# Down projection of a two-layer decoder step: low parts of the weights on VectorE, sums read out one item earlier, additions spread over two products

## The reference

```
def ffn(x, norm_g, w_gu, w_down):
    h = rmsnorm(x, norm_g)
    g, u = jnp.split(h @ w_gu, 2, axis=-1)
    return x + (jax.nn.silu(g) * u) @ w_down
```

## Time and profile before

| | us |
|---|---|
| median of three runs (lowest, highest) | 2724.93 (2722.43, 2726.48) |
| profiled execution | 2711.63 |
| its span, first to last instruction | 2710.0 |
| TensorE matmul busy | 2627.9 (97%) |
| VectorE busy | 1598.3 (59%) |
| ScalarE busy | 1131.1 (42%) |
| GpSimd busy | 1248.2 (46%) |
| mean granted TensorE clock | 0.997 |

### The profile page before, as it was taken

The page is one execution under the profiler, slowest core; times in us unless marked ns, Lnnn a source line. Parts: engine busy times, 40 slices in busy tenths (PEclk is TensorE's granted clock), DMA queues, the critical chain, the costliest instruction groups (busy, mean ns, idle before and its releaser), DMA issues.

```text
span 2710.0 us, 51112 instructions
## 1 busy us (share of the span) xinstructions
PE 2627.9 (97%) x20404; PEld 2371.3 (88%) x20404; DVE 1598.3 (59%) x2435; ACT 1131.1 (42%) x2373; POOL 1248.2 (46%) x986
## 2 busy tenths in 40 slices
PE   8999999999999999999999999999999999999998
PEld 6866667666679899999999999978999999999998
DVE  3222257776563666766668861285376667666875
ACT  4022213666551644444433342175264444434335
POOL 2431000222232488778744651236257787775452
PEclk9999999999999999999999999999999999999999
DMA  7754310310433232322375331200322223228433
GB/s 231 207 166 154 92 32 12 105 33 2 137 110 138 69 101 84 113 93 93 101 261 182 85 90 41 54 2 17 105 68 98 97 85 117 93 95 309 134 83 104
DMA packets 256590, 283.78 MB, mean 105 GB/s; under 512 B 43098, under 2 KB 192655, under 8 KB 255506
## 3 DMA queue, kind: packets, MB, share of 16 engines
q1 hardware_dynamic: 245840, 247.84, 29.1%
q0 software_dynamic: 7616, 30.14, 3.6%
q10 hardware_dynamic: 2898, 2.54, 0.3%
HBM read 214.25 MB, written 71.32 MB: 105 GB/s over the span
## 4 chain that ended last, share of the span: by engine, by line
PE 63%; DVE 7%; issue 1%; ACT 1%; POOL 1%; DMA 1%; SPq 0%; DVEq 0%; ACTq 0%; POOLq 0%
PE ps L2541 32%; PE ps L3114 13%; PE ps L2342 8%; PE ps L2358 3%; DVE d_blo L3058 2%; DVE arena L3072 1%; PE ps L3438 1%; PE ps L3298 1%; PE ps L3419 1%; DVE part L2701 1%; PE ps L3402 1%; PE ps L2010 1%; PE ps L1998 1%; PE ps L2045 0%; DMA arena<-in_w_gate_up 0%
## 5 line engine op out<-in xcount | busy, mean ns | idle before, releaser
L2541 PE MATMUL ps<-part,block_hi 128*128 128x272 f32 x4768 | 793.6, 289 | 10.8 <-DVE spare_sb L2763 6.4
L2541 PEld LDWEIGHTS ps<-part,block_hi 128*128 128x128 f32 x4768 | 677.5, 189 | 11.6 <-DVE spare_sb L2763 6.8
L2541 PE MATMUL ps<-part,block_lo 128*128 128x272 f32 x2672 | 532.1, 290 | 0.0
L2829 POOL TENSOR_TENSOR block_lo<-arena,block_hi 128x512 fp32r<-128x512 f32 x296 | 443.7, 1529 | 53.4 <-ACT block_hi L2596 46.8
L2541 PEld LDWEIGHTS ps<-part,block_lo 128*128 128x128 f32 x2672 | 410.1, 190 | 1.0 <-issue 1.0
L3063 POOL TENSOR_TENSOR d_wlo<-arena,d_whi 128x512 fp32r<-128x512 f32 x154 | 248.0, 1630 | 249.5 <-ACT d_whi L3054 249.3
L3114 PE MATMUL ps<-d_bhi,d_whi 128*128 128x272 f32 x1232 | 258.3, 291 | 23.4 <-DVE arena L3201 12.8
L3114 PE MATMUL ps<-d_blo,d_whi 128*128 128x272 f32 x1232 | 256.5, 289 | 0.0
L3114 PE MATMUL ps<-d_bhi,d_wlo 128*128 128x272 f32 x1232 | 255.7, 289 | 0.0
L633 PE MATMUL ps<-arena 128*128 128x352 f32 (+1 forms) x768 | 240.8, 471 | 0.0
L2596 ACT CAST block_hi<-arena 128x512 fp32r<-128x512 f32 x296 | 167.1, 618 | 147.6 <-POOL arena L2844 86.1
(11 more groups left out here) (518 smaller groups left out, 4670.9 us busy)
## 6 DMA issues: line engine op xcount, KB each, us to landing
arena<-in_w_gate_up SPq DMA_DIRECT2D x176, 256.0 KB, 3.8
spare_sb<-a_keep SPq DMA_DIRECT2D x78, 272.0 KB, 2.8
arena<-a_keep SPq DMA_DIRECT2D x64, 272.0 KB
arena<-in_w_down SPq DMA_DIRECT2D x16, 1024.0 KB, 6.3
a_keep<-arena SPq DMA_DIRECT2D x58, 272.0 KB, 2.1
arena<-in_cache_nsa_slc_kv SPq DMA_DIRECT2D x112, 128.0 KB, 2.5
a_keep<-spare_sb SPq DMA_DIRECT2D x52, 272.0 KB, 2.0
arena<-in_cache_nsa_cmp_kv SPq DMA_DIRECT2D x109, 128.0 KB, 2.3
```

Source lines behind the costliest of these rows:

```text
L2541: mm = nc.tensor.matmul(ps[:, b + j, 0:QT], y, z[:, j * QT:(j + 1) * QT], start=first and m == 0, stop=last and m == 2)
L2829: p.tensor_tensor(block_of(q, "lo", a), block_f[q % 2]["lo", a], block_of(q, "hi", a).bitcast(F32), ALU.subtract).then_inc(sem("up_lo"), 1)
```

## The change

`low_w` takes the engine as an argument. GpSimd makes the low parts of the weights of items 0 to 5 alone; from item 6 on VectorE makes them, each right after the low part of the item's activations. VectorE evicts quads 0 and 1 after item j == 2 and quads 2 and 3 after item j == 3 of the next product; the weight sums of j = 1, 2, 3 are put off until these evictions are issued. ScalarE's copies of P1's banks move from j = 3, 4 to j = 2, 3. Two of the four `v_buf` pieces are now halves of `gate_even[0]`. Of the twelve `add_v`, four stay in P5 (j = 5 to 8, one each) and eight move to P3 (j = 5 to 8, two each). ScalarE's last four scalings and VectorE's four `low` move from between items 72 to 75 to behind the last item.

```
--- before.py
+++ after.py
@@ -2887,7 +2887,7 @@
         D_BANKS = (6, 0, 2, 4)
         D_SEGS, D_SEGS_LAST = ((0, 3), (3, 6), (6, 9), (9, PAIRS)), ((0, 3), (3, 6), (6, PAIRS))
         place = {"11": h0 + 12672, "21": h0 + 18304, "12": h0 + 23936}
-        v_buf = [rstd[:][:, 0:HT], rstd[:][:, HT:T], t2_buf, t3_buf]
+        v_buf = [rstd[:][:, 0:HT], rstd[:][:, HT:T], gate_even[0][:, 0:HT], gate_even[0][:, HT:]]
         stage_odd = [spare_sb[:, T:T + HT], spare_sb[:, T + HT:2 * T]]
 
         def stage(n):
@@ -3057,10 +3057,10 @@
             dve.wait_ge(*high_done("b", l, n))
             nc.vector.tensor_tensor(entry(n)[1], stage(n), entry(n)[0].bitcast(F32), ALU.subtract).then_inc(sem("d_blo"), 1)
 
-        def low_w(pool, l, n):
+        def low_w(e, engine, l, n):
             name, j = item(n)
-            pool.wait_ge(*high_done("w", l, n))
-            nc.gpsimd.tensor_tensor(entry(n)[3], stay(D_STAYS[name], j), entry(n)[2].bitcast(F32), ALU.subtract)\
+            e.wait_ge(*high_done("w", l, n))
+            engine.tensor_tensor(entry(n)[3], stay(D_STAYS[name], j), entry(n)[2].bitcast(F32), ALU.subtract)\
                 .then_inc(sem("d_wlo"), 1)
 
         def sum_w(e, engine, l, n):
@@ -3072,8 +3072,8 @@
             engine.tensor_tensor(stay(dst, j), stay(a, j), stay(b, j), op).then_inc(sem("d_sum"), 1)
 
         def down_pool(pool, l):
-            for n in range(ITEMS):
-                low_w(pool, l, n)
+            for n in range(RING):
+                low_w(pool, nc.gpsimd, l, n)
 
         SQUARES = [(u, 0) for u in range(QUADS)] + [(u, 1) for u in range(QUADS, KC)] + [(u, 1) for u in range(QUADS)] \
             + [(u, 0) for u in range(QUADS, KC)]
@@ -3145,11 +3145,11 @@
                 high_b(act, l, n)
                 high_w(act, l, n)
                 i, j = n // PAIRS, n % PAIRS
-                if i == 1 and j in (3, 4):
-                    if j == 3:
+                if i == 1 and j in (2, 3):
+                    if j == 2:
                         act.wait_ge(sem("up_a"), FC * (l + 1))
-                        act.wait_ge(*kept_z(l, PAIRS))
-                    for q in (range(QUADS - 1), (QUADS - 1,))[j - 3]:
+                        act.wait_ge(*kept_even(l, 0, EVENS[0]))
+                    for q in (2 * (j - 2), 2 * (j - 2) + 1):
                         act.wait_ge(*quad_done(l, 0, q))
                         nc.scalar.copy(two(v_buf[q]), product_banks(q)).then_inc(sem("d_copied"), 1)
                 if i in (2, 5) and 6 <= j < 10:
@@ -3160,8 +3160,8 @@
                     act.wait_ge(*item_used(l, LAST0 - 1))
                     for u in range(QUADS):
                         scaled(u, slice(0, T))
-                if n >= LAST0 + RING and n < LAST0 + RING + QUADS:
-                    scaled(QUADS + n - LAST0 - RING, slice(HT, T))
+            for u in range(QUADS, KC):
+                scaled(u, slice(HT, T))
 
             def finish(k):
                 act.wait_ge(*evicted(l, len(D_ORDER) - 1, k))
@@ -3189,6 +3189,8 @@
                     dve.wait_ge(*x_again(l, 0))
                 if name == "P7" and q == 0:
                     dve.wait_ge(*x_again(l, 1))
+                if name == "P5" and q == 0:
+                    dve.wait_ge(*x_again(l, 2))
                 if name == "P1":
                     dve.wait_ge(*copied(l, q))
                 if name == "P6":
@@ -3201,12 +3203,11 @@
                     ins = v.tensor_tensor(x, x, got, ALU.subtract if name == "P4" else ALU.add)
                 ins.then_inc(sem("d_evict"), 1)
 
-            def add_v(k):
-
-                q, (u, half) = k // 3, ((k // 3, 1), (QUADS + k // 3, 0), (QUADS + k // 3, 1))[k % 3]
-                if k == 0:
+            def add_v(q, u, half):
+
+                if u == 0:
                     dve.wait_ge(*x_again(l, 2))
-                dve.wait_ge(*evicted(l, 3, q))
+                dve.wait_ge(*evicted(l, 4 if u < QUADS else 3, q))
                 x = x_half(u, half)
                 v.tensor_tensor(x, x, v_buf[q], ALU.add).then_inc(sem("d_vadd"), 1)
 
@@ -3228,24 +3229,39 @@
                 v.scalar_tensor_tensor(out=h_lo[u], in0=xT[:, u], scalar=cols[:, g0 + u:g0 + u + 1],
                                        in1=h_hi[u].bitcast(F32), op0=ALU.mult, op1=ALU.subtract).then_inc(sem("h_lo"), 1)
 
-            for n in range(3, ITEMS):
-                low_b(dve, l, n)
+            def sums(n):
                 if 2 * PAIRS <= n + SUM_LEAD < LAST0:
                     dve.wait_ge(*low_done("w", l, n + SUM_LEAD - PAIRS))
                     sum_w(dve, v, l, n + SUM_LEAD)
+
+            for n in range(3, ITEMS):
+                low_b(dve, l, n)
+                if n == RING:
+                    dve.wait_ge(*low_done("w", l, RING - 1))
+                if n >= RING:
+                    low_w(dve, v, l, n)
                 i, j = n // PAIRS, n % PAIRS
+                if i == 0 or j not in (1, 2, 3):
+                    sums(n)
                 if i == 0 and 3 <= j < 7:
                     sum_pair(dve, l, PAIRS - 1, j - 3)
+                if i and j == 2:
+                    if i == 5:
+                        dve.wait_ge(*reached("d_vadd", 3 * QUADS * l + QUADS))
+                    if i == 6:
+                        dve.wait_ge(*reached("d_vadd", 3 * QUADS * (l + 1)))
+                    evict(i - 1, 0)
+                    evict(i - 1, 1)
                 if i and j == 3:
-                    if i == 5:
-                        dve.wait_ge(*reached("d_vadd", 3 * QUADS * (l + 1)))
-                    for q in range(QUADS - 1):
-                        evict(i - 1, q)
-                if i and j == 4:
-                    evict(i - 1, QUADS - 1)
-                if i == 4 and j >= 5:
-                    for k in range(2 * (j - 5), 2 * (j - 4)):
-                        add_v(k)
+                    evict(i - 1, 2)
+                    evict(i - 1, 3)
+                    for m in range(n - 2, n + 1):
+                        sums(m)
+                if i == 4 and 5 <= j < 5 + QUADS:
+                    add_v(j - 5, QUADS + j - 5, 1)
+                if i == 5 and 5 <= j < 5 + QUADS:
+                    add_v(j - 5, j - 5, 1)
+                    add_v(j - 5, QUADS + j - 5, 0)
                 if i in (2, 5) and j == 9:
                     for e in range(3):
                         add_square((0 if i == 2 else QUADS) + e)
@@ -3254,8 +3270,8 @@
                 if n == LAST0 + RING - 1:
                     for e in range(2 * QUADS, 3 * QUADS):
                         add_square(e)
-                if not l and n >= LAST0 + RING and n < LAST0 + RING + QUADS:
-                    low(n - LAST0 - RING)
+            for u in range(0 if l else QUADS):
+                low(u)
             if l:
                 final_dve(dve, E, evict, add_square)
             else:
```

## The result

The changed kernel takes 2693.26 us (median of 4, 2689.35 to 2696.84), the kernel before 2723.68 (median of 4, 2718.95 to 2726.48; three of them are those behind the 2724.93 above): ratio 0.989, interval 0.987 to 0.991, faster by 30.4 us, or 1.1%. The profiled executions tell another tale: 2692.93 us (one of the four) against 2711.63 before (none of its four), 18.7 less, where I had said 2691.6. Both differences need their reason.

What follows compares the result with a forecast made beforehand. TensorE, 97% busy, bounds the kernel; only its stalls and lower-clock time can be won. Savings of 7.4 (layer 0) and 12.6 us (layer 1), 20.0 off median 2724.9, give 2704.9; range 2701 to 2709, with rivals 2694 to 2715.

Steps and rivals of the forecast that it cites:

- Low parts of the weights: Both down projections: with 71 of 77 per layer off GpSimd, VectorE's extra work fits, 29 us of P3's 33.3.
- Rival C: P7 to P3: VectorE becomes the bound, its operations averaging 1.0 us; slower, about 2785 us; chance 0.05.
- Start of the stage: First items of each down projection: GpSimd stops after item 5, saving 2.2 us in layer 0, 0.8 in layer 1.
- Changes of product: Between products of both down projections: the evictions' idle time goes, saving 8.5 us in layer 0, 8.3 in layer 1.
- rival B: Changes of product keep half their stalls, quad 0's eviction waiting behind item 2's low weights; 8.9 us saved, 2716; chance 0.15.
- End of layer 0: Item 76: GpSimd's next panel holds up VectorE; TensorE idles 5.0 us, not 3.6, losing 1.4, plus 2.7 at half clock.
- rival A: End of layer 0: the panel lands too late to hurt, gaining 3.6 and keeping the clock; 27.7 saved, 2697.2 us; chance 0.22.
- The sum: Both down projections: 7.4 us saved in layer 0 and 12.6 in layer 1, 20.0 together; profiled execution 2711.6 to 2691.6.
- the transfer: From profile to timed runs: stalls are the same work in both, so 20.0 comes off the median 2724.9, giving 2704.9.
- one half-clock stretch: Layer 1's down projection: 6 us at 1.2 GHz follow a stall that goes, saving 2.7 us.

Runs made afterwards that it cites:

- e8: The kernel before, unchanged, profiled once more: span 2711.3 us at a clock of 0.995.
- e3: The kernel before with only the low weights from item 6 on moved to VectorE, evictions as they were: 2700.54 us, ratio 0.9945.
- e4: The kernel before with only evictions and ScalarE's copies of P1 earlier and weight sums put off, low weights still on GpSimd: 2700.45 us, ratio 0.9941.
- e2: The changed kernel with a GpSimd wait that never held, so in effect the changed kernel again: 2694.61 us, ratio 0.991 to the kernel before.
- e7: The changed kernel again, unchanged: 2693.81 us beside 2717.39 for the kernel before, ratio 0.992.
- e6: The changed kernel with the first panel's `w_lo` split into two GpSimd operations: 2693.40 us, ratio 0.9906 to the kernel before.
- e1: The kernel before again, no edit: 2718.61 us (median of 12), ratio 1.0004; profile span 2718.0 at a clock of 0.993.
- e5: The changed kernel, but GpSimd waits for layer 0's item 76 low weights before splitting the next projection's first panel: 2692.69 us, ratio 0.9909 to the kernel before.
- e9: e5 with all eight `low` behind the last additions of squares and P4's four evictions ahead of those additions: 2686.54 us, ratio 0.9894 to the kernel before.
- e10: e5 with all eight `low` behind the last additions of squares, evictions not reordered: 2686.51 us, ratio 0.9882 to the kernel before.

## Why the prediction was right in its parts and wrong in its time

*Low parts of the weights:* right. Operations at 0.69 and 0.72 us, no item late between the first six and P4. Rival C needed 0.72 us per operation from start to start in P3; VectorE was busy for 27.5 us of P3's 33.5 with 44 operations in the trace, 0.63 each.

*Start of the stage:* right. 2.38 us of idle time in layer 0 became 0.23 (2.2 less forecast), 0.6 in layer 1 became 0.2. But this stall is not the same in each execution: the unchanged kernel had 0.54 there in e8.

*Changes of product:* right in size and cause; rival B fell. e3 and e4 add that I priced two parts as one chain where each alone suffices.

*End of layer 0:* right in size and cause, with one operation off. A stall of 5.0 us forecast, 4.9 measured; half clock behind it; 1.1 us of idle time before the next projection, as before. I had `w_hi` hold item 75's low weights; it came some 0.5 us later than in my chain and held item 76's first low part, and the end is the same, since `w_lo` still went ahead of the last one. It holds in the three traces of the kernel with this ending (4.9 in the result, 4.9 in e2, 4.6 in e7), so rival A's margin was not used up once. The Trainium skill's rule in "SBUF — State Buffer", section "SBUF: two separate sides", an exclusive lock held for the whole instruction, is the one that I had weighed. The trace agrees (0.57 and 0.55 us after GpSimd's operations), and so does e6: half the operation, 2.1 us less of the stall.

*The sum:* 20.0 us forecast for the profiled execution, 18.7 measured; 19 to 20.5 at equal clock; 21.5 and 23.6 between the medians of the two repeats. One slip in it moves nothing: 1848 matmuls at 25.90 / 204 us are 234.6 us, not 233, and layer 1's stage now takes 234.6.

*The step that failed* is the transfer: "That execution is 13.3 us below the median of the runs; the stalls are the same work in both, so I take the difference off the median". It treats 2724.9 as the level of the kernel before, and the 13.3 us as something that stays. Neither holds. The 56 later executions of the kernel before have a median of 2716.6, 8.3 us lower; less 20.0 that would have been 2696.6. The other 3.3 us of my error of 11.6 lie in the price of the stalls, which are about the same idle time in each execution but not the same cost. The profile of before had a clock of 0.997, and paid for one half-clock stretch in the two stages, 2.7 us in my sum; e1 paid for five. The two stages take 495.3, 501.3 and 494.4 us in the three profiles, 497.0 on average, against 474.4 in both of the changed kernel that I measured (the result and e7): 22.6, within the 21.5 to 23.6 of the repeats. That average rests on e1 alone; without it, it would be 20.4. That a stall which goes takes its chance of a half clock along fits the higher mean clock of the changed kernel, but no run separates this from the half-clock stretches of the other stages, which vary too.

*What stays open:* the larger part of the error, the 8.3 us, and with it the first comparison's 30.4 us. Its four executions of the kernel before (2718.95 to 2726.48) are all as slow as the slowest 19 of the 56 later ones; four drawn from these at random would be so about once in a hundred times, and their clocks are not known. In the three later comparisons the median was 2716 to 2717, while the changed kernel was no different (2693.26 first, 2694.61 and 2693.81 later). The first interval (0.987 to 0.991) and e7's (0.9899 to 0.9941) meet only at their ends, so I take 21 to 24 us as the better measure of the change and leave the other 7 to 9 unexplained. Also open is what decides whether a stall is followed by the half clock.

## What to carry to other kernels

Before taking a forecast off a median, compare the profiled execution's clock and time with the timed ones, and compare executions of both kernels at equal clock: a median of three was 8 us off the level of 56, and at equal clock the forecast difference was right. When work leaves an engine that shares a port, ask what that engine starts next and how long its operations are. Here an operation was waited for whole, so put evictions, which read PSUM and ran at 0.72 us throughout, ahead of what needs the port, and keep the other engine's long operations away from the moment at which a short one is urgent. Removing one wait (e5) or halving it (e6) gained nothing, because the next wait in the same queue grew; taking out both gained some 7 us (e9, e10).

## What the hardware showed that I had not expected

Stalls of 2.23, 2.41 and 2.52 us were followed by the 1.2 GHz clock in e1, and one of 1.95 us in e10, while stalls of 3.05 and 3.38 us were not in the first profile; I found nothing in the rows around them that tells the cases apart. Executions of the same program took from 2708.66 to 2728.46 us. And VectorE did 142 operations more in less busy time (1583.5 us against 1598.3), since most of the waits for the port that its durations held are gone: a low part of activations from `spare_sb` took 1.05 us on average over the whole kernel before, and 0.72 from 1420 to 1560 us now.
